# One unmasked product for eight SSD heads in place of a product per head

## The reference, cut to what matters

```python
a_cs = jnp.cumsum(a, axis=-1)                     # a = dt * A, per head
decay_in = jnp.exp(segsum(a))                     # exp(a_cs[l] - a_cs[s]) where s <= l, else 0
CB = jnp.einsum('bclgn,bcsgn->bgcls', Cc, Bc)     # one per group of 8 heads
y_diag = jnp.einsum('bgrcls,bcsgrp->bclgrp', CB[:, :, None] * decay_in, Xdt)
y = y_diag + y_off + X * D_skip                   # y_off is 0 with one chunk
y = y * silu(z)                                   # then an RMS norm over each group of 512 columns
```

## Time and profile before

| | |
|---|---|
| device time, median of 3 runs | 543.5 us (543.46 to 543.78) |
| span of the profiled execution | 541.4 us |
| own device time of the profiled execution | not given apart; the runs lie 2.1 us above its span |
| TensorE busy | 531.4 us, 98% |
| DVE, ACT, POOL busy | 434.0, 341.2, 61.3 us |
| chain that ended last | 93% of it TensorE |

### The profile page before, as it was taken

One profiled execution on the slowest core, in us unless ns is written; L12 is line 12 of the kernel. 1 busy time (PEld: TensorE's weight loads), 2 busy tenths in 40 slices (PEclk: granted clock), 3 DMA queues, 4 the chain that ended last, 5 costly groups with the idle time before them and its releaser, 6 DMA issues.

```text
span 541.4 us, 9714 instructions
## 1 busy us (share of the span) xinstructions
PE 531.4 (98%) x3633; PEld 489.3 (90%) x3633; DVE 434.0 (80%) x661; ACT 341.2 (63%) x559; POOL 61.3 (11%) x99
## 2 busy tenths in 40 slices
PE   8999999999999999999999999999999999999995
PEld 6999999999999979998888788899999999999994
DVE  6899988888887784877768756779898898888845
ACT  6866646655654664867988864675665655656534
POOL 2002000000000210442741102000000000000014
PEclk9999999999999999999999999999999999999998
DMA  9867766565874417568526244527674467765302
GB/s 269 303 234 243 232 205 221 178 187 197 269 233 157 144 36 216 160 214 282 197 84 227 79 157 155 157 79 253 215 247 151 158 219 232 232 184 178 104 0 79
DMA packets 69966, 99.70 MB, mean 184 GB/s; under 512 B 1941, under 2 KB 55393, under 8 KB 69938
## 3 DMA queue, kind: packets, MB, share of 16 engines
q1 hardware_dynamic: 68336, 94.48, 53.3%
q0 software_dynamic: 1456, 4.59, 2.5%
q10 hardware_dynamic: 146, 0.27, 0.1%
HBM read 98.27 MB, written 1.06 MB: 183 GB/s over the span
## 4 chain that ended last, share of the span: by engine, by line
PE 93%; DVE 2%; ACT 1%; issue 1%; SPq 1%; DMA 1%; POOL 1%; POOLq 0%; ACTq 0%; DVEq 0%
PE bank L1734 29%; PE bank L1735 29%; PE bank L1736 29%; DMA x<-in_x 1%; PE bank L1882 1%; PE bank L2029 1%; PE bank L2030 1%; PE bank L2028 1%; SPq L415 1%; PE bank L2069 1%; DVE x L1189 0%; SPq L406 0%; PE bank L2080 0%; PE bank L2081 0%; PE bank L2044 0%
## 5 line engine op out<-in xcount | busy, mean ns | idle before, releaser
L1734 PE MATMUL bank<-hT_hi,w_hi 128*128 128x256 f32 x736 | 208.6, 283 | 0.0
L1736 PE MATMUL bank<-hT_hi,w_lo 128*128 128x256 f32 x736 | 208.3, 283 | 0.0
L1735 PE MATMUL bank<-hT_lo,w_hi 128*128 128x256 f32 x736 | 208.2, 283 | 0.0
L1165 DVE TENSOR_TENSOR w_lo<-raw,w_hi 128x1024 fp32r<-128x1024 f32 x126 | 154.1, 1226 | 21.1 <-ACT w_hi L666 20.5
L666 ACT ACTIVATE w_hi<-raw 128x1024 fp32r<-128x1024 f32 x126 | 132.2, 1056 | 47.7 <-DMA raw<-in_ffn_w 26.5
L1734 PEld LDWEIGHTS bank<-hT_hi,w_hi 128*128 128x128 f32 x736 | 141.1, 192 | 2.0 <-issue 0.5
L1735 PEld LDWEIGHTS bank<-hT_lo,w_hi 128*128 128x128 f32 x736 | 141.1, 192 | 1.3
L1736 PEld LDWEIGHTS bank<-hT_hi,w_lo 128*128 128x128 f32 x736 | 141.1, 192 | 0.0
L1734 PE MATMUL bank<-w_hi,hT_hi 128*128 128x512 f32 (+1 forms) x176 | 66.0, 375 | 1.6 <-DVE hT_lo L1244 0.9
L1736 PE MATMUL bank<-w_hi,hT_lo 128*128 128x512 f32 (+1 forms) x176 | 63.7, 362 | 0.0
L1735 PE MATMUL bank<-w_lo,hT_hi 128*128 128x512 f32 (+1 forms) x176 | 63.5, 361 | 0.0
(11 more groups left out here) (254 smaller groups left out, 825.1 us busy)
## 6 DMA issues: line engine op xcount, KB each, us to landing
raw<-in_ffn_w SPq DMA_DIRECT2D x54, 1024.0 KB, 5.5
raw<-in_w_in SPq DMA_DIRECT2D x16, 1024.0 KB, 5.6
kv_tok<-in_ffn_w SPq DMA_DIRECT2D x10, 1024.0 KB, 5.8
raw<-in_w_out SPq DMA_DIRECT2D x6, 1024.0 KB, 4.9
x<-in_x SPq DMA_DIRECT2D x4, 256.0 KB, 4.0
kv_tok<-in_ffn_w SPq DMA_DIRECT2D x4, 256.0 KB, 4.8
z_silu<-in_ffn_w SPq DMA_DIRECT2D x4, 256.0 KB, 5.2
norm_w<-cs_heads POOLq DMA_DIRECT2D x2, 512.0 KB, 5.0
```

The source lines that it names most:

```text
L1165: dve.tensor_tensor(lo, src, hi, ALU.subtract).then_inc(half_ready, 1)
L1734: pe.matmul(dst, lhs[0], rhs[0], start=start, stop=False, skip_group_check=True)
L1735: pe.matmul(dst, lhs[0], rhs[1], start=False, stop=False, skip_group_check=True)
L1736: return pe.matmul(dst, lhs[1], rhs[0], start=False, stop=stop, skip_group_check=True)
```

## The change

For early keys s and late queries l, exp(a_cs[l] - a_cs[s]) is split at the last early token e into exp(a_cs[e] - a_cs[s]) and exp(a_cs[l] - a_cs[e]). The first goes, with dt, into a weighted copy of x (`cross_x`), the second onto the result. What is left in the middle, the block of CB, is the same for all eight heads of a group, so it is one product of 128 x 128 with 128 x 512 for a group.

- DVE, step 19: six small subtractions for both exponents, after all four loads of the sums. ACT, step 20: one small Exp for both.
- ACT and DVE for each head: 128 + 128 columns in place of 256 + 128. PE for each head: two products in place of three.
- POOL: weights x for group 0 ahead of the rotation of the queries, for group 1 behind it; adds the cross part of group 0 to `normed` ahead of the rotation of the keys, that of group 1 behind it.
- PE: the product of group 0 after the heads of step 22, that of group 1 after those of step 26, into the banks 4 and 5. DVE scales the results into `xbc` at steps 23 and 27.
- DVE's add of a group's late rows waits for POOL's add; the transposes of the first group's rows wait for DVE's scaling of group 1, which frees bank 5.

```diff
+        def cs_turns():
+            for h0, place in ((0, norm_w[:, :, :]), (8, normed[:, :, 0:512]), (12, z_silu[:, :, 512:1024])):
+                rows = place.rearrange("p t (h l) -> p t h l", l=SEQ)
+                yield slice(h0, h0 + (4 if h0 else 8)), rows[:, :, :, P - 1]
+        def cross_x(g):
+            return xbc[:, 2 * g:2 * g + 2, :].rearrange("p c l -> p (c l)")
+        def cross_y(g):
+            return xbc[:, 2 * g + 4:2 * g + 6, :].rearrange("p c l -> p (c l)")
...
+            def cross_weigh(g):
+                heads = slice(8 * g, 8 * g + 8)
+                if g == 0:
+                    pool.wait_ge(cross_exp, 1)
+                    step(pool.tensor_tensor(dts[:, 1, 0, :], dts[:, 0, 0, :], dts[:, 6, 0, :], ALU.mult))
+                pool.tensor_tensor(by_head(cross_x(g)), by_head(x_tok[:, 0, 512 * g:512 * g + 512]),
+                                   dts[:, 1, 0, heads].unsqueeze(2).to_broadcast([P, 8, SP_]), ALU.mult).then_inc(cross_x_ready, 1)
+            def cross_add(g):
+                pool.wait_ge(cross_scaled, g + 1)
+                y = normed[:, 1, D_ATTN + 512 * g:D_ATTN + 512 * (g + 1)]
+                pool.wait_ge(skip_ready, 2 * g + 2 if g else 3)
+                pool.tensor_tensor(y, cross_y(g), y, ALU.add).then_inc(cross_added, 1)
+            cross_weigh(0)
             pool.wait_ge(consts_loaded, 16)
             pool.wait_ge(proj_out, 4)
             rotate(q_tok)
+            cross_weigh(1)
+            cross_add(0)
             pool.wait_ge(proj_out, 6)
             rotate(k_tok)
+            cross_add(1)
...
-                    for s, (a, b) in enumerate(((0, 256), (256, 384))):
-                        act.activation(decay[:, h % 2, a:b], cs_row(h)[:, s * P:], ACT.Relu,
+                    for s in range(TT):
+                        own = slice(s * P, (s + 1) * P)
+                        act.activation(decay[:, h % 2, own], cs_row(h)[:, own], ACT.Relu,
                                        bias=dts[:, 7, s, h:h + 1], scale=-1.0).then_inc(decay_arg, 1)
...
+            def cross_decays():
+                act.wait_ge(cross_arg, 6)
+                act.activation(dts[:, 0, :, :], dts[:, 0, :, :], ACT.Exp).then_inc(cross_exp, 1)
...
+            def cross_arguments():
+                for j in range(4):
+                    dve.wait_ge(cs_loaded[j], 16)
+                for heads, turn in cs_turns():
+                    before, after = (dts[:, 7, s, heads].rearrange("p (t h) -> p t h", t=TT) for s in range(TT))
+                    dst = [dts[:, 0, s, heads].rearrange("p (t h) -> p t h", t=TT) for s in range(TT)]
+                    dve.tensor_tensor(dst[0], turn, before, ALU.subtract).then_inc(cross_arg, 1)
+                    dve.tensor_tensor(dst[1], after, turn, ALU.subtract).then_inc(cross_arg, 1)
+            def cross_scale(g):
+                dve.wait_ge(cross_done, g + 1)
+                e = dts[:, 0, 1, 8 * g:8 * g + 8].unsqueeze(2).to_broadcast([P, 8, SP_])
+                dve.tensor_tensor(by_head(cross_y(g)), by_head(bank[:, 4 + g, :]), e, ALU.mult).then_inc(cross_scaled, 1)
...
+                    if t:
+                        dve.wait_ge(cross_added, g + 1)
...
+                if m in (23, 27):
+                    cross_scale(m // 4 - 5)
                 if m == 25:
                     ssd_gate(0)
...
-                pe.matmul(bank[:, 7, o], m[:, P:SEQ], x_tok[:, 0, c], start=True, stop=False)
-                pe.matmul(bank[:, 7, o], m[:, SEQ:SEQ + P], x_tok[:, 1, c], start=False, stop=True).then_inc(y_done, 1)
+                pe.matmul(bank[:, 7, o], m[:, P:SEQ], x_tok[:, 1, c], start=True, stop=True).then_inc(y_done, 1)
+            def ssd_cross(g):
+                pe.wait_ge(cross_x_ready, g + 1)
+                pe.matmul(bank[:, 4 + g, :], cb[:, g, P:SEQ], cross_x(g), start=True, stop=True).then_inc(cross_done, 1)
...
+                if m in (22, 26):
+                    ssd_cross((m - 22) // 4)
                 if m == 22:
                     qk_transposes(q_tok, 2, 2)
                 if m == 26:
                     qk_transposes(k_tok, 0, 4)
                 if m == 27:
-                    mix_transposes(0, D_ATTN, cb_ready, 2)
+                    mix_transposes(0, D_ATTN, cross_scaled, 2)
```

More of the change, by code:

```diff
@@ L302, in build @@
         m_ready = sem("m_ready")
+        cross_arg = sem("cross_arg")
+        cross_exp = sem("cross_exp")
+        cross_x_ready = sem("cross_x_ready")
+        cross_done = sem("cross_done")
+        cross_scaled = sem("cross_scaled")
+        cross_added = sem("cross_added")
         y_done = sem("y_done")
@@ L326, in cs_row, with by_head @@
             return normed[:, t, c:c + SEQ] if h < 12 else z_silu[:, t, 512 + c:512 + c + SEQ]
+        def cs_turns():
[6 more added lines that the diff above has]
+            return xbc[:, 2 * g + 4:2 * g + 6, :].rearrange("p c l -> p (c l)")
+        def by_head(t):
+            return t.rearrange("p (h d) -> p h d", d=SP_)
         def cols_half(t, half):
@@ L1013, in decay_exp @@
                     act.wait_ge(decay_arg, 2 * (h + 1))
-                    act.activation(decay[:, h % 2, :], decay[:, h % 2, :], ACT.Exp, scale=-1.0).then_inc(decay_ready, 1)
+                    both = decay[:, h % 2, 0:SEQ]
+                    act.activation(both, both, ACT.Exp, scale=-1.0).then_inc(decay_ready, 1)
+            def cross_decays():
+                act.wait_ge(cross_arg, 6)
+                act.activation(dts[:, 0, :, :], dts[:, 0, :, :], ACT.Exp).then_inc(cross_exp, 1)
             def square_mix(col, first_col, count):
@@ L1090, in _ @@
                 if m == 20:
+                    cross_decays()
                     for t in range(TT):
@@ L1597, in weigh @@
                 dve.wait_ge(decay_ready, h + 1)
-                for s, (a, b) in enumerate(((0, 256), (256, 384))):
-                    dve.scalar_tensor_tensor(mix_m[:, h % 2, a:b], cb[:, g, a:b], dts[:, 6, s, h:h + 1],
-                                             decay[:, h % 2, a:b], ALU.mult, ALU.mult).then_inc(m_ready, 1)
+                for s in range(TT):
+                    own = slice(s * P, (s + 1) * P)
+                    dve.scalar_tensor_tensor(mix_m[:, h % 2, own], cb[:, g, 2 * s * P:(2 * s + 1) * P], dts[:, 6, s, h:h + 1],
+                                             decay[:, h % 2, own], ALU.mult, ALU.mult).then_inc(m_ready, 1)
+            def cross_arguments():
[10 more added lines that the diff above has]
+                dve.tensor_tensor(by_head(cross_y(g)), by_head(bank[:, 4 + g, :]), e, ALU.mult).then_inc(cross_scaled, 1)
             def ssd_add(g):
@@ L1680, in _ @@
                     weigh(2 * (m - 20) + 1)
+                if m == 19:
+                    cross_arguments()
+                if m in (23, 27):
+                    cross_scale(m // 4 - 5)
                 if m == 25:
```

## The result

The changed kernel takes 546.44 us at the median of six runs (545.26 to 547.49), beside 543.65 for the kernel before on the same chips: 2.79 us more, ratio 1.0051, 95% interval 1.0039 to 1.0062. It is slower, and by more than the range allowed (545.6). The profiled execution has a span of 545.0 us.

A forecast was written before the change was run, and what follows sets the result against it. TensorE (PE), busy 98% of the span, was taken to bound the kernel. PE gains 1.84 us, then stands still for 2.24, net +0.40: forecast 543.9 us, range 542.8 to 545.6.

The forecast's parts named there:

- the moved step: On POOL, group 1's add now waits for DVE's scaling, ahead of two loads and group 0's row factors; their 5 us margin goes.
- the edits costed at nothing: Shorter decays, six small DVE subtractions, a small Exp and POOL's two weightings of x (1.38 us each): taken to cost nothing.
- W: Time at which DVE ends weighting head 15: taken as 288.55 us, with bounds of 288.23 and 289.19.
- the clock: PE's clock could drop from 2.4 to 1.2 GHz after a 2.2 us stand; counted within Rival 1, 22% together.
- PE's own gain: PE alone: sixteen fewer products save 3.56 us, two new ones cost 0.86 each, so -1.84 us.
- The rival of 1.71 for a product: Each new 512-column PE product costs 1.71 us and delays the key transposes: net +1.2 us, 544.7 us; chance 8%.
- The chain behind W: DVE scaling, POOL add, two load issues, row factors, DVE scalings, PE transposes: W + 6.65 = 295.20 us, PE standing 2.24.
- the meeting of the two engines: POOL makes the second factor while DVE scales group 0's first half; contention moves the end by 0.3 us either way.
- the second factor: POOL's row factor for the second half of group 0: taken as 1.2 us, between 0.9 not held and 1.5 held.
- Rival 1: POOL is held longer by its two DMA issues, up to 1.15 us: 545.1 to 546.0, named 545.4; 22% with the clock.

## Why the prediction was wrong

The direction of the surprise was named, as the moved step, and its chain was the right one. The forecast of 543.9 had it as a draw with PE's gain; 546.4 is a clear loss: +2.79 in place of +0.40. Two steps failed: the edits costed at nothing, which held PE up at head 1 and so put W late, and the clock, which was given no term. The steps, against the profiled execution:

- **PE's own gain** was right within 0.1: the new products take 0.91 each and not 0.86 (from start to start, in TensorE's timeline above), so -3.56 + 1.82 = -1.74. With both waits removed the kernel gains 1.5 us. The rival of 1.71 for a product falls.
- **The chain behind W** was right. From the end of head 15's weighting (289.35 + 1.14 = 290.49) to the start of the second half's transposes (296.56) it takes 6.07; the prediction had 6.21. The scaling, the add, both issues, the factors and the meeting of the two engines stand in the rows almost as they were added up: the second factor took 1.27 (294.45 to 295.72), between its bounds, the power 0.91 beside DVE's scaling.
- **W itself** was 289.75 with the start of the execution taken off, not 288.55, and above its upper bound of 289.19. Here the step "Edits that I cost at nothing" failed. It looked at whom POOL's weighting of x delays on POOL, and not at DVE, which was working at the same time. The meeting of the engines was known from the earlier trace rows, and was used only at the end of the chain. PE lost 0.73 at head 1 (the next product starts 0.95 after the one before, not 0.22), and all that follows, W too, came later by as much. The rest of the 1.20 is waits of DVE for ACT, 0.28 and 0.32, of which the sum had kept half, and small shifts. (Eight times 0.13 is 1.05, not the 1.08 of the sum; that is 0.03 of it.)
- **The clock** was named and given no term; it was put inside another rival's range. Between the second transposes and the first scores PE takes 1.19 us longer than at full clock, from start to start: 0.35 in the transposes (0.77 to the projection, 0.42 in the kernel with PE kept busy) and 0.84 in the projection (3.77 to the first scores, 2.93 before). By the runs it is 1.0. The projection's start and the first scores, in the timeline of the kernel before, and the first scores of the changed one, whose projection starts at 297.33:

```profile
294.56 0.48 PE L1734 MATMUL bank<-w_hi,hT_hi 128*128 128x512 f32 x1
...
297.49 0.49 PE L2059 MATMUL bank<-kT,qT 64*128 64x128 f32 x4
```

```profile
301.10 0.49 PE L2138 MATMUL bank<-kT,qT 64*128 64x128 f32 x4
```

- **The refill** of PE after a wait was left out: four transposes that start after a wait take 0.65 from the first start to the last end at full clock (at 295.83 in the kernel with PE kept busy), and the sum had 0.44, from transposes that follow on without one: 0.21 us.

The sum mended: 0.40 as forecast, + 1.20 for W, - 0.14 for the chain, + 0.21 for the refill, + 1.19 for the clock = 2.86. The trace has the first scores here:

```profile
301.17 0.42 PE bank L2138 x4
```

In the chain that ended last they stand at 301.17 against 297.56; less 0.74 that is 2.87 later, and the runs say 2.79. Most of the mended terms are read from this same execution, so that they add up shows that nothing large is left out, and not what caused each; that rests on the experiments.

Rival 1 named the right sign and a time of 545.4 by the wrong mechanism: POOL goes on 0.07 us after an issue. The Trainium skill, in DMA: Bandwidth & Descriptors, Latency and other measured facts, gives about 1 us to the first byte of a DMA by way of GpSimd, as the overhead of emitting descriptors. It is not what POOL's list loses here for an issue, which is 0.59 and 0.56.

The Trainium skill says in GPSIMD Engine Reference, Specifications, that GpSimd shares its SBUF interfaces with VectorE, with contention where a VectorE instruction has two SBUF inputs. The trace agrees, at head 1 (2.80 us against 1.13) more than at the place where it was cited (a second factor of 1.27, between the 0.9 of the free rows and 1.5).

What stays open: how much of the runs' spread of the changed kernel (545.3 to 547.5) is the clock; the execution with the lowest time has the highest mean granted clock, 0.997 against 0.994 to 0.995. The same stands in the kernel before with the moved step: 546.16 at 0.997, and 547.58 to 547.93 at 0.994. Both fit executions in which the clock stayed up, but those are not the profiled ones, so it is not shown.

## What to carry to other kernels

When a step with a new wait is put into an engine's list, look first at what stands behind it in that list, and for whom: here a 1.7 us gain in arithmetic was lost mainly to two small row factors queued behind an add that did not need to come first. For each added operation on POOL look at what DVE does in the same microseconds, and for each new stand of PE ask whether the granted clock survives it; the stand costs its length and then the slow stretch behind it.

## What the runs showed of the hardware

- After a stand of PE of 1.75 us (recorded wait 1.58) the granted clock fell to 0.50 while the first four transposes behind it ran (0.75 in 295.6 to 295.8, 0.50 in 295.8 to 296.0), ahead of the second stand, and stayed there for some 3 us; with two stands of recorded waits of 0.5 us each it stayed at 1.00.
- DVE and POOL hold each other up: four weightings on DVE take 2.80 us in place of 1.13 beside the D_skip products and the weighting of x on POOL, and POOL's power takes 0.91 beside DVE's scaling, 0.57 ahead of it. Small operations are caught too: a subtraction on 128 x 4 took 0.16 us with POOL idle (the changed kernel) and 1.01 where a D_skip product had begun at 257.15 (the kernel with these products by group). Not every one is: the subtraction ahead of it there, at 257.19, took 0.15. DVE's timelines, first the changed kernel's:

```profile
257.52 0.16 DVE L1663 TENSOR_TENSOR dts<-dts,normed 128x4 f32<-128x4 f32 x1
```

```profile
257.26 1.01 DVE L1663 TENSOR_TENSOR dts<-dts,normed 128x4 f32<-128x4 f32 x1
```
